# Half of the second projection's input weights loaded during the mLSTM phase, into one 64 KB area that four phases use in turn

## The reference

```python
def adaln(c, w, b):
    mod = jax.nn.silu(c) @ w + b
    ...
# layer 0
hn = rmsnorm(x, a_g_norm) * (1 + scale) + shift
q_a, c_new, kr_new, mq, mk, mv, mi, mf, mo, z = split_cols(hn @ a_w_in, IN_A_SIZES)
o_mla = chunk_causal_attention(q, k, v, pos, kpos)
(C1, n1, m1), hs = lax.scan(mlstm_chunk, init, xs)
x = x + gate * (concatenate([o_mla, hm]) * silu(z)) @ a_w_out
# layer 1
hn = rmsnorm(x, c_g_norm) * (1 + scale) + shift
qkv, a, bb, z = split_cols(hn @ c_w_in, IN_C_SIZES)      # 3072 + 8 + 8 + 1024 columns
conv = causal_conv4(qkv); q, k, v = split(silu(conv))
o = gated_delta_rule(q, k, v, g, beta)
x = x + gate * (rmsnorm(o, g_out) * silu(z)) @ c_w_out
```

## Time and profile before

| what | value |
|---|---|
| median of 3 runs | 3728.23 us (3727.15 to 3731.6) |
| the profiled execution, its own time | 3726.34 us |
| span of its trace | 3724.7 us |
| PE busy | 3494.0 us (94%) |
| DVE, ACT, POOL busy | 1645.3 us (44%), 1058.8 us (28%), 421.9 us (11%) |
| `project_c` begins (first instruction of SP's list) | 1969.45 us |
| L1975, the blocks of the second projection, PE busy | 723.0 us |

### The profile page before, as it was taken

The page is one execution under the profiler, slowest core; times in us unless marked ns, Lnnn a source line. Parts: engine busy times, 40 slices in busy tenths (PEclk is TensorE's granted clock), DMA queues, the critical chain, the costliest instruction groups (busy, mean ns, idle before and its releaser), DMA issues. The chain is left out here.

```text
span 3724.7 us, 46810 instructions
## 1 busy us (share of the span) xinstructions
PE 3494.0 (94%) x17697; PEld 2136.8 (57%) x17697; DVE 1645.3 (44%) x2850; ACT 1058.8 (28%) x2739; POOL 421.9 (11%) x565
## 2 busy tenths in 40 slices
PE   6999999999879999979993999999999988799998
PEld 3555555555357777755552555555554568666765
DVE  3222222222235555545541543444444348478784
ACT  1121121122135545421112233232321355222322
POOL 0000000000010000000000100000000012344442
PEclk9999999999969999989995999999999998799999
DMA  8522222121254100033316111121111158755552
GB/s 286 164 77 64 65 81 64 62 80 56 53 146 113 31 21 21 10 127 113 113 63 229 38 53 54 58 62 47 50 43 44 55 168 244 221 166 149 164 153 83
DMA packets 349361, 362.17 MB, mean 97 GB/s; under 512 B 129475, under 2 KB 277678, under 8 KB 346990
## 3 DMA queue, kind: packets, MB, share of 16 engines
q1 hardware_dynamic: 307414, 306.49, 27.6%
q10 hardware_dynamic: 35112, 30.37, 2.7%
q0 software_dynamic: 6640, 22.68, 2.1%
HBM read 231.45 MB, written 128.01 MB: 97 GB/s over the span
## 5 line engine op out<-in xcount | busy, mean ns | idle before, releaser
L1975 PE MATMUL d_bank<-d_hT,d_w_in 128*128 128x512 f32 (+1 forms) x1920 | 723.0, 533 | 8.4 <-DMA d_w_in<-in_c_w_in 4.9
L545 PE MATMUL a_bank<-a_w_in,a_hT 128*128 128x512 f32 (+1 forms) x1296 | 564.5, 592 | 0.0
L1975 PEld LDWEIGHTS d_bank<-d_hT,d_w_in 128*128 128x128 f32 x1920 | 338.3, 194 | 351.0 <-issue 337.8
L545 PEld LDWEIGHTS a_bank<-a_w_in,a_hT 128*128 128x128 f32 (+1 forms) x1296 | 241.6, 189 | 287.4 <-issue 287.2
L1073 PE MATMUL c_ps<-c_kT,c_q 96*128 96x512 f32 (+3 forms) x576 | 236.1, 540 | 15.6 <-DMA c_q<-scratch_qT 15.6
L2111 DVE SCALAR_TENSOR_TENSOR d_cv<-d_xb,k_wconv,d_cv 128x512 f32<-128x512 f32 (+1 forms) x360 | 236.9, 658 | 12.8
L1983 PE MATMUL d_bank<-d_w_in,d_hT 128*128 128x344 f32 (+3 forms) x864 | 238.3, 439 | 0.0
L2800 PE MATMUL r_bank<-k_w_next,r_mixT 128*128 128x512 f32 x512 | 237.0, 612 | 0.0
L2109 DVE TENSOR_SCALAR d_cv<-d_xb,k_wconv 128x512 f32<-128x512 f32 (+1 forms) x120 | 52.9, 441 | 390.5 <-ACT d_xb L2050 383.1
L1517 PE MATMUL m_bank<-m_w_out,m_mixT 128*128 128x512 f32 x512 | 222.6, 593 | 0.0
L1983 PEld LDWEIGHTS d_bank<-d_w_in,d_hT 128*128 128x128 f32 (+1 forms) x864 | 150.1, 184 | 74.9 <-issue 4.8
(11 more groups left out here) (377 smaller groups left out, 4630.5 us busy)
## 6 DMA issues: line engine op xcount, KB each, us to landing
k_n_kv<-scratch_qkv SPq DMA_DIRECT2D x17, 1024.0 KB, 5.0
scratch_qkv<-d_ts SPq DMA_DIRECT2D x64, 256.0 KB, 2.3
a_w_ada<-in_c_w_ada SPq DMA_DIRECT2D x16, 768.0 KB
d_w_in<-in_c_w_in ACTq DMA_DIRECT2D x6, 2048.0 KB, 17.1
l_kT<-scratch_g_kT SPq DMA_DIRECT2D x17, 512.0 KB, 5.5
l_qT<-scratch_g_qT SPq DMA_DIRECT2D x17, 512.0 KB, 6.0
k_n_kT<-scratch_g_kT SPq DMA_DIRECT2D x17, 512.0 KB, 6.4
r_qT<-scratch_g_qT SPq DMA_DIRECT2D x17, 512.0 KB, 8.2
```

The source lines that it names most:

```text
L545: mm = nc.tensor.matmul(o[:n, 0:w], hT[u][:, k, :n], weights[:, k, at:at + w], start=(k == 0), stop=(k == KD - 1))
L1975: mm = nc.tensor.matmul(o[:, 0:w.w], w_in[:, k, w.a * P:(w.a + 1) * P], hT[w.r % 2][:, k, 0:w.w], start=(k == 0), stop=(k == KD - 1))
```

## The change

One tile `big` of 64 KB a partition is allocated at the start and freed after `project_c`. `setup`'s two weight pieces, 2048 columns of `project_a`'s weight, `attend`'s keys and four parts of `c_w_in` lie in it one after the other. The keys are held as four tiles of 512 columns and a small one for the sample's new keys, so each load of the sample's past keys becomes two transfers. Four of the seven parts of `c_w_in` (columns 0 to 2047, 8 MB) are now issued by SP in `mlstm`, one each in its rounds 2 to 5, and SP waits for them at the phase's end; ACT issues the other three (2, 2 and 4.06 MB) ahead of its fifth norm, and its wait for row tiles 0 to 2 at the start is gone. `project_c`'s own tile `w_in` shrinks by the 2048 columns.

```diff
@@ class Modulation
-        self.w = [ctx.enter_context(nc.sbuf_tensor(f"{pre}wada{j}", [P, KD, D], F32)) for j in range(2)]
+        self.w = [K["big"][:, j * KD * D:(j + 1) * KD * D].rearrange("p (k n) -> p k n", n=D) for j in range(2)]
+BIG = 16384
+W_EARLY = 4 * 512
+def w_early(K):
+    return [K["big"][:, j * KD * 512:(j + 1) * KD * 512].rearrange("p (k n) -> p k n", n=512) for j in range(W_EARLY // 512)]
@@ project_a
-        w_in = sb("w_in", [P, KD, W_A - C_MQ])
+        w_z1 = sb("w_z1", [P, KD, 512])
+        w_two = {c0: K["big"][:, i * KD * 1024:(i + 1) * KD * 1024].rearrange("p (k n) -> p k n", n=1024)
+                 for i, c0 in enumerate((C_MQ, C_MO))}
@@ attend
-        kT = sb("kT", [MASKED, H, SEQ + DEC])
+        groups_kT = [K["big"][:, g * 512 * H:(g + 1) * 512 * H].rearrange("p (h n) -> p h n", n=512) for g in range(4)]
+        new_kT = sb("new_kT", [DQ, H, DEC])
...
-                sp.dma_start(kT[0:DQ, hs, PAST:2 * PAST], sc["pkT"][:, hs, :]).then_inc(s_keys_in[c], 16)
-                sp.dma_start(kT[0:DQ, hs, 2 * PAST:], sc["kT"][:, hs, SEQ:SEQ + DEC]).then_inc(s_keys_in[c], 16)
+                for g in range(2):
+                    sp.dma_start(groups_kT[2 + g][0:DQ, hs, :], sc["pkT"][:, hs, g * 512:(g + 1) * 512]).then_inc(s_keys_in[c], 16)
+                sp.dma_start(new_kT[:, hs, :], sc["kT"][:, hs, SEQ:SEQ + DEC]).then_inc(s_keys_in[c], 16)
@@ mlstm, SP's list
             for t in range(TILES):
+                if t >= 2 and t - 2 < W_EARLY // 512:
+                    c0 = (t - 2) * 512
+                    sp.dma_start(w_early(K)[t - 2],
+                                 io["c_w_in"][:, c0:c0 + 512].rearrange("(k p) n -> p k n", p=P)).then_inc(next_w_in, 16)
                 if t + RING < TILES:
                     done(sp, "C", t)
...
             sp.wait_ge(out_stored, 16 * 10)
+            sp.wait_ge(next_w_in, 16 * (W_EARLY // 512))
@@ project_c
-        w_in = sb("w_in", [P, KD, W_C])
+        w_in = sb("w_in", [P, KD, W_C - W_EARLY])
-        parts = [(c, c + 4 * P) for c in range(0, GC, 4 * P)] + [(GC, W_C)]
+        parts = [(c, c + 4 * P) for c in range(W_EARLY, GC, 4 * P)] + [(GC, W_C)]
+        def weights(k, c0, c1):
+            return early_w[c0 // 512][:, k, c0 % 512:c0 % 512 + c1 - c0] if c1 <= W_EARLY else w_in[:, k, c0 - W_EARLY:c1 - W_EARLY]
...
-                    if w.r == 0:
-                        pe.wait_ge(w_sem[w.a // 4 if w.kind == "block" else -1], 16)
+                    if w.r == 0 and (w.kind == "z" or w.a * P >= W_EARLY):
+                        pe.wait_ge(w_sem[(w.a * P - W_EARLY) // (4 * P) if w.kind == "block" else -1], 16)
...
-            for k in range(AHEAD):
-                x_loaded(act, k)
-            load_w(0)
...
                     if w.k == FEW - 1:
-                        load_w(1, 2, last, *range(3, last))
+                        load_w(*range(len(parts)))
```

More of the change, by code:

```diff
@@ L431, in columns @@
         def columns(c0):
-            return (w_lat, c0) if c0 < C_MQ else (w_in, c0 - C_MQ)
+            for start in w_two:
+                if start <= c0 < start + 1024:
+                    return w_two[start], c0 - start
+            return (w_lat, c0) if c0 < C_MQ else (w_z1, c0 - C_Z - 512)
         def lanes(name, t):
@@ L456, in _ @@
                 s0 = D_MQ if name == "mlstm" else c0
-                sp.dma_start(w_in[:, :, c0 - C_MQ:c1 - C_MQ],
+                sp.dma_start(columns(c0)[0][:, :, 0:c1 - c0],
                              io["a_w_in"][:, s0:s0 + c1 - c0].rearrange("(k p) n -> p k n", p=P)).then_inc(part_in[name], 16)
@@ L1005, in _ @@
                 nc.gpsimd.memset(q[u][DQ:MASKED, :, 64:P], 0.0).then_inc(q_set, 1)
[L1006 to L1009, removed]
+            for g in range(4):
+                blocks = groups_kT[g][DQ:MASKED, :, :].rearrange("p h (b n) -> p h b n", n=P)
+                nc.gpsimd.memset(blocks[:, :, :, 0:64], 0.0).then_inc(mask_set, 1)
+                nc.gpsimd.memset(blocks[:, :, :, 64:P], -1e30).then_inc(mask_set, 1)
             put(zr[:, :], 0.0, 1)
@@ L1072, in scores @@
                         if e > a:
-                            mm = nc.tensor.matmul(ps[:, o:o + e - a], q[k % 2][0:DQ, h, :], kT[0:DQ, h, a:e], start=True, stop=True)
+                            mm = nc.tensor.matmul(ps[:, o:o + e - a], q[k % 2][0:DQ, h, :], keys_of(DQ, h, a, e), start=True, stop=True)
                         if b > e:
-                            mm = nc.tensor.matmul(ps[:, o + e - a:o + b - a], q[k % 2][:, h, :], kT[:, h, e:b], start=True, stop=True)
+                            mm = nc.tensor.matmul(ps[:, o + e - a:o + b - a], q[k % 2][:, h, :], keys_of(MASKED, h, e, b), start=True, stop=True)
                     mm.then_inc(scored, 1)
@@ L1974, in _ @@
                     for k in range(KD):
-                        mm = nc.tensor.matmul(o[:, 0:w.w], w_in[:, k, w.a * P:(w.a + 1) * P], hT[w.r % 2][:, k, 0:w.w],
+                        mm = nc.tensor.matmul(o[:, 0:w.w], weights(k, w.a * P, (w.a + 1) * P), hT[w.r % 2][:, k, 0:w.w],
                                               start=(k == 0), stop=(k == KD - 1))
@@ L1983, in _ @@
                             mm = nc.tensor.matmul(o[lane:lane + n, 0:a1 - a0], hT[w.r % 2][:, k, w.a * P:w.a * P + n],
-                                                  w_in[:, k, GC + a0:GC + a1], start=(k == 0), stop=(k == KD - 1))
+                                                  weights(k, GC + a0, GC + a1), start=(k == 0), stop=(k == KD - 1))
                     mm.then_inc(filled[w.bank], 1)
@@ L2004, in _ @@
         def _(act):
-            last = len(parts) - 1
             def load_w(*which):
@@ L3108, in build @@
             K[n] = K[n][:, :]
+        middle = ExitStack()
+        keep(middle, {"big": [P, BIG]})
         with ExitStack() as first:
@@ L3122, in build @@
             run(attend, mlstm)
-        run(project_c)
+        with middle:
+            run(project_c)
         keep(ctx, {"gg": [P, T1, GH], "sx": [P, T1, 3, GH], "nk": [P, T1, GH], "bk": [P, T1, GH], "eq": [P, T1, GH],
```

13 lines of the change are left out of this document (8 added, 5 removed).

## The result

The changed kernel takes 3698.83 us (median of 4 runs, 3696.49 to 3700.9) against 3729.91 us before (4 runs, 3727.15 to 3732.6): ratio 0.9917, 95% interval 0.9899 to 0.9934, so 31 us faster, with an interval of 25 to 38. The forecast was 3702. The profiled execution after has a span of 3699.3 us against 3724.7, 25.4 us less.

The account below looks back on a forecast made before the run. PE, busy 94% of the span, bounds the kernel, so only its waits at project_c's start can be won: 5.7 + 20.3 = 26.0 us, 3726.3 - 26.0 = 3700.3, as a median 3702; own range 3697 to 3707, 8-in-10 range 3697 to 3714.

Parts of the forecast that it names:

- the sum: Whole kernel: 5.7 us at the first block plus 20.3 from ACT's issues, 26.0 us gained, everything else zero.
- Block 0: Start of project_c: PE's first block begins at about 1981.1 instead of 1986.83, 5.7 us earlier.
- the wait on part 0: Start of project_c: the first block no longer waits for its weights, worth 2.6 us.
- the row tiles: Start of project_c: ACT's first norm needs row tile 0 alone and comes 3.1 us earlier.
- ACT's issues: Ahead of ACT's fifth norm in project_c: three issues costing 20.22 us go, three costing 4.9 stay; gain 20.3 us.
- The Trainium skill: Cited against two steps: issue time usually small, gain 5.7 us alone; 2 us per transfer, two extra in attend 4 us.
- first rival: project_c: only the wait on part 0 goes, ACT is held all the same, 3722.5 us; 8% together with a middle case.
- The clock: Start of the wide blocks: same slow-clock price as before, zero net, bounded by +2.9 and -2.8 us.
- `mlstm`: Four 2 MB issues on SP's queue cost 0: a part takes 9.4 us, 12.7 us are spare.
- slower rival: mlstm, SP's queue: parts landing in 20.0 us make four tiles 7.3 us late each, +29 us, 3731 us; chance 4%.
- `attend`: Past-key loads split into 2 KB pieces ahead of an awaited query tile: cost 0, between -0.9 and +2 us.
- its two bounds: Favourable ends: -2.8 us if the clock is already up at the wide blocks, -0.9 us for attend's split key loads.

Follow-up runs that it names:

- experiment 9: Changed kernel with ACT's wait for row tiles 0 to 2 put back ahead of its first norm, no issue behind it: 3703.91 us.
- experiments 2, 3 and 4: experiment 2, experiment 3, and the kernel before with parts 3 to 5 loaded as one issue in wide 6 KB pieces, the last 3714.21 us.
- experiment 2: Changed kernel with only parts 1 to 3 loaded early; ACT's first wait and issue of part 0 put back: 3711.48 us.
- experiment 3: Kernel before, no early load, ACT's last three weight issues spread behind its copies of wide blocks 3, 7 and 11: 3707.8 us.
- experiment 1: Changed kernel with only part 0 loaded early; ACT issues parts 1 to 3 before its fifth norm in the earlier order: 3721.85 us.
- Experiment 8: Changed kernel with all four early parts issued in one round of mlstm instead of one in each of four rounds: 3711.66 us.
- experiment 5: Changed kernel with each half of the heads' past keys in attend as one transfer of 4 KB pieces instead of two: 3705.26 us.
- experiment 10: Changed kernel, weight loads moved past the fifth norm, third and fourth query tiles issued earlier on SP in attend: 3684.17 us.

## Why the prediction was right

The mechanism and the sum held: 26.0 us forecast for the phase, 26.4 and 26.3 measured.

**Block 0.** Forecast 5.7 us earlier, 2.6 of it from the wait on part 0 and 3.1 from the row tiles. Measured 6.15, with 3.05 from the row tiles (experiment 9) and 3.1 left for part 0; by the block's place in the other three kernels that waited for both (16.8, 17.0 and 17.1 us of the phase in experiments 2, 3 and 4, against 14.27) part 0 is 2.5 to 2.9. The 0.4 us that the forecast lacked lies in front of the first norm, which it put at 5.30 us of the phase (1974.75 - 1969.45) and which came at 4.93. The issue of its row tile, and the landings of the stretch in KB and us:

```profile
1972.41 8.43 SPq L1912 DMA_DIRECT2D d_x<-scratch_x  x5
...
d_x<-scratch_x SPq DMA_DIRECT2D x1, 256.0 KB, 3.7
```

The tile landed in 3.7 us instead of 3.8, at 1976.11, and that is where the norm starts: the quarter of a microsecond that the prediction allowed for the semaphore is shown by no run.

**ACT's issues.** Forecast 20.3 us, measured 20.29. That the three early ones would cost 4.9 in the same place was right as well (4.93), though for a reason that the prediction had only by half: it said that an issue is held while what was issued before drains, and took it for enough that the three sizes are the same and the queue is empty. What counts is the pieces that have yet to go through. With the same megabytes in the order 4, 2, 2 the same number of pieces stands in the queue, but the ones in front are twice as large; the cost is 10.3 us (experiment 2), and the forecast would have been 5 us off. It held since the three issues that stay have the order of the rows it was read from.

**The Trainium skill** (DMA: Bandwidth & Descriptors, "Issuing engines are not separate DMA queues") holds the sequencer's time for an issue to be usually small beside the transfer. Here 20.22 us stood on the path, and moving them to another place gave 19.6 us back (experiment 3). The prediction's first rival, 3722.5 with ACT held all the same, is close to what experiment 1 measures, where the issues were left: 3721.85.

**The clock.** Forecast zero net at the wide blocks. The stretches from 2010 on in the changed kernel, the granted clock being the third number from the end, answer to the earlier trace rows:

```profile
2010.00:2015.00 5.00, 1.48 (x4) 0.60 (x3) 0.94 (x4) 3.05 (x9) 0.00 (x0) 0.50 1.03 417
2015.00:2020.00 5.00, 5.00 (x9) 2.09 (x8) 0.00 (x0) 0.00 (x0) 0.00 (x0) 0.68 1.03 418
2020.00:2025.00 5.00, 5.00 (x25) 3.30 (x24) 1.01 (x2) 0.60 (x1) 0.54 (x2) 1.00 0.05 21
```

Back at 2.4 GHz within 6 us of the first wide block, as before; ACT's first copy of a wide block stands 9.2 us behind its start instead of 9.9, a gain of 0.7, inside the bounds. A price that the forecast did not have stands in `mlstm`, at its fourth tile: the granted clock is 0.50 from 1641 to 1644 and back at 1.00 from 1647 on, before it was 0.75 from 1640 to 1643 and 1.00 from 1643 on, against the same work. It cost 0.87 us in the one execution and 0.30 in the other. It is not the early loads, since SP issued the first part only later:

```profile
1663.32 0.43 SPq L1455 DMA_DIRECT2D k_big<-in_c_w_in  x1
```

The stretch takes 75.62 us before, and 76.08 and 77.83 in experiments 3 and 4, whose `mlstm` is the same as before.

**`mlstm`.** Forecast 0, from 9.4 us a part and 12.7 to spare. The landings after (two issues each, KB, median us):

```profile
k_big<-in_c_w_in SPq DMA_DIRECT2D x2, 2048.0 KB, 11.3
...
k_m_vx<-scratch_ym SPq DMA_DIRECT2D x2, 256.0 KB, 12.1
```

The part takes 11.3 us instead of the 9.4 that it took alone on ACT's queue. SP issues 1.5 MB of other transfers right ahead of it (the prediction counted 1 MB), and the load behind it 12.1 instead of 7.4: 4.7 us later, with 12.7 to spare. The rounds keep their 19.57 us. Experiment 8 shows that the cover is real and finite: with 8 MB ahead PE waits 7.98 us, once. The slower rival had the right place, but its price for a part was wrong: 20.0 us were taken from a queue that was backed up, and a part took 11.3.

**`attend`.** Forecast 0, between -0.9 and +2; the first profile said +2.40, beyond that end. The step that was wrong is the bound, not the value: it was made from two rates inside one execution, and the stretch varies by 8 us between executions of the same instructions (experiment 5). Nothing smaller can be forecast or judged there from one profile. The Trainium skill's 2 us for each transfer (SBUF - State Buffer, section on the DMA setup-cost knee), 4 us here, are neither shown nor refuted by these eleven profiles.

**The total.** 25.40 and 27.10 between profiled executions, 31 between medians. The profiled execution before took 3726.34 us, 3.6 below the median of the four runs, and the one after is the slowest of its four, 2.1 above their median: this is the 5.6 us between 25.4 and 31. The forecast took the difference between execution and median for 1.9 us on both sides; the 3702 was 3 us too high, and in which stretch the runs gain more than the profiles stays open. The lower end of its own range, 3697, is a little below what its two bounds add up to (3702 - 2.8 - 0.9 = 3698.3); the measured 3698.83 lies above both.

## What to carry to other kernels

When the profile shows "issue" ahead of an engine that others wait for, look at its DMA issues first: move them to a place where the queue is empty, or give them fewer and larger pieces, the largest last, before memory is spent on loading earlier. In a shared queue a load that is wanted soon goes ahead of those that are wanted later; what stands in front is paid in full once the spare time is used up. And before a microsecond in a DMA-bound stretch is charged to a change, profile the same kernel twice.

## What the runs showed of the hardware

In the loads of the second projection's weight an issue was held until some 2,250 to 2,550 pieces were left in its queue, in ACT's and in SP's, whatever the bytes; ACT's first two issues of each row, 2048 pieces together, took 0.4 and 0.7 to 0.8 us. The stretches, from the first issue to the end of the last:

```
kernel (queue)            issues  pieces issued  gone   left   MB left
changed (ACT)                  3           3072   529   2543       7.4
issues spread (ACT)            3           3072   561   2511       7.3
parts 1 to 3 (ACT)             3           3072   826   2246       5.0
part 0 only (ACT)              4           4096  1630   2466       7.2
part 0 only (ACT)              6           6144  3678   2466       5.2
before (ACT)                   6           6144  3594   2550       5.3
wide pieces (ACT)              4           4096  1608   2488      11.5
one round (SP)                 8           4608  2199   2409       5.1
```

The lowest count belongs to the kernel whose first load has the 4160-byte pieces; why it is 200 lower stays open.

The count is not a limit for every load. In `attend` of the kernel before, SP's queue holds pieces of 256 bytes to 4 KB. This issue was held too, and of the 5440 pieces issued from 1016.29 to its end the queue's count has these gone:

```profile
1033.95 10.58 SPq L984 DMA_DIRECT2D c_v<-scratch_v  x1
...
q1 hardware_dynamic: 3978, 6.23, 96.6%
```

Some 1,500 were left, and some 1,850 of 3200 at the end of the first held issue there (4.47 us from 1019.76 on the earlier trace rows). What sets the number is open.

With the gap in `attend` filled (experiment 10) the granted clock is back at 1.00 by 1065, while in the changed kernel it stays at 0.50 until 1080, ten microseconds after PE took up work again at 1070.30. The first turned output behind that place comes 19.3 us earlier (1065.65 against 1084.96), but 0.9 of that was there already at the turned output ahead of it (1044.70 against 1045.61). Of the other 18.4 us 17.05 are the wait: it cost its own length and some 1.4 us more, in a stretch in which the clock stayed at 0.50 for longer.
